# x loaded a second time in turned layout, and the inverse norms spread over rows, in a fused decoder-block kernel

## What is computed

```python
u = rms_norm(h, norm_w[layer])            # x * rsqrt(mean(x*x) + eps) * w
proj = jnp.einsum('bsd,dc->bsc', u, w_in[layer])
hg_q, hg_f, hg_i, hg_z, at_q, at_k, at_v, at_z = jnp.split(proj, split_points, axis=-1)
...
o_hg = hgrn2_mixer(hg_q, hg_f, hg_i, lb); o_hg = rms_norm per head * silu(hg_z)
o_at = mixture of three dilated_window_attention(q, k, v) * silu(at_z)
h = h + einsum(concat([o_hg, o_at]), w_out)
return rms_norm(h, final_norm_w)
```

## Time and profile before

| | us |
|---|---|
| median of 3 runs | 1277.51 |
| lowest, highest | 1275.31, 1278.64 |
| the profiled execution, its own time | 1280.67 |
| its span, first to last instruction | 1278.9 |

### The profile page before, as it was taken

The page is one execution under the profiler, slowest core; times in us unless marked ns, Lnnn a source line. Parts: engine busy times, 40 slices in busy tenths (PEclk is TensorE's granted clock), DMA queues, the critical chain, the costliest instruction groups (busy, mean ns, idle before and its releaser), DMA issues.

```text
span 1278.9 us, 24337 instructions
## 1 busy us (share of the span) xinstructions
PE 1248.3 (98%) x8944; PEld 1090.0 (85%) x8944; DVE 704.3 (55%) x1933; ACT 460.3 (36%) x1328; POOL 436.2 (34%) x441
## 2 busy tenths in 40 slices
PE   7999999999999999999999999999999998999997
PEld 7989999999999989999888888888888876888886
DVE  5847877887766797111455444544554545333332
ACT  5631222222222212112555555554554546421121
POOL 5543254343534413122153345333533434021000
PEclk8999999999999999999999999999999998999999
DMA  6520122211221212341455466545545666544431
GB/s 213 175 90 19 55 63 81 77 59 59 63 79 59 75 67 76 96 116 48 125 141 141 122 143 152 134 116 148 147 125 140 161 179 181 160 145 143 148 116 66
DMA packets 121717, 143.94 MB, mean 113 GB/s; under 512 B 20352, under 2 KB 86400, under 8 KB 121600
## 3 DMA queue, kind: packets, MB, share of 16 engines
q1 hardware_dynamic: 117024, 134.26, 36.9%
q10 hardware_dynamic: 4576, 8.13, 2.3%
HBM read 87.56 MB, written 29.62 MB: 92 GB/s over the span
## 4 chain that ended last, share of the span: by engine, by line
PE 88%; DVE 3%; DMA 3%; issue 1%; POOL 1%; ACT 1%; SPq 1%; ACTq 0%; POOLq 0%; DVEq 0%
PE bank L665 11%; PE bank L667 11%; PE bank L666 11%; PE bank L837 6%; PE bank L836 6%; PE bank L835 6%; PE bank L863 5%; PE bank L865 5%; PE bank L864 5%; PE bank L927 3%; PE bank L936 3%; PE bank L991 3%; PE bank L998 3%; PE bank L760 2%; PE bank L964 2%
## 5 line engine op out<-in xcount | busy, mean ns | idle before, releaser
L665 PE MATMUL bank<-w_hi,u_hi 128*128 128x256 f32 x768 | 221.3, 288 | 3.3 <-DVE u_lo L1472 2.4
L666 PE MATMUL bank<-w_lo,u_hi 128*128 128x256 f32 x768 | 218.2, 284 | 0.0
L667 PE MATMUL bank<-w_hi,u_lo 128*128 128x256 f32 x768 | 218.1, 284 | 0.0
L665 PEld LDWEIGHTS bank<-w_hi,u_hi 128*128 128x128 f32 x768 | 148.1, 193 | 5.1 <-DVE u_lo L1472 3.9
L666 PEld LDWEIGHTS bank<-w_lo,u_hi 128*128 128x128 f32 x768 | 148.2, 193 | 0.1
L667 PEld LDWEIGHTS bank<-w_hi,u_lo 128*128 128x128 f32 x768 | 148.1, 193 | 0.0
L1472 DVE TENSOR_TENSOR room<-room 128x256 f32<-128x256 f32 (+6 forms) x386 | 130.9, 386 | 16.7 <-POOL room L1357 10.7
L835 PE MATMUL bank<-u_hi,w_hi 128*128 128x512 f32 x256 | 107.8, 421 | 0.5 <-issue 0.5
L1472 DVE TENSOR_TENSOR t<-bank,tab 128x512 f32<-128x512 f32 x64 | 42.4, 684 | 116.6 <-DMA tab<-in_rope 52.7
L836 PE MATMUL bank<-u_lo,w_hi 128*128 128x512 f32 x256 | 101.9, 398 | 2.7 <-DMA far_v<-values 2.7
L665 PE MATMUL bank<-u_hi,w_hi 128*128 128x512 f32 x256 | 103.0, 402 | 0.6 <-ACT sg_tile L1093 0.6
(11 more groups left out here) (169 smaller groups left out, 2846.9 us busy)
## 6 DMA issues: line engine op xcount, KB each, us to landing
qd<-turned SPq DMA_DIRECT2D x64, 256.0 KB, 4.5
stage<-in_w_groups SPq DMA_DIRECT2D x42, 256.0 KB, 4.0
room<-in_x SPq DMA_DIRECT2D x16, 512.0 KB, 3.9
values_gates<-vg_tile SPq DMA_DIRECT2D x64, 128.0 KB, 1.7
room<-values_gates SPq DMA_DIRECT2D x16, 512.0 KB, 3.9
tab<-in_rope SPq DMA_DIRECT2D x16, 512.0 KB, 4.5
wide<-mix_weights SPq DMA_DIRECT2D x32, 256.0 KB, 3.9
xr<-in_x SPq DMA_DIRECT2D x16, 512.0 KB, 4.9
```

The lines of the kernel that those rows point to most:

```text
L665: yield nc.tensor.matmul(dst, lhs_hi(k), rhs_hi(k), start=(k == 0), stop=False)
L666: yield nc.tensor.matmul(dst, lhs_hi(k), rhs_lo(k), start=False, stop=False)
L667: last = nc.tensor.matmul(dst, lhs_lo(k), rhs_hi(k), start=False, stop=(k == KT_N - 1))
```

## The change

The host hands x over a second time, turned: tile by tile, the 128 features of a group over the partitions and 128 positions along the row (`x_turned`). The kernel loads both. x itself is only squared and summed. The turned x goes into three slots `xT` of two tiles each, four tiles one by one (`load_turned`), and the other twelve as pairs of 1 MB (`load_pair`). TensorE no longer turns x. Instead `spread_norms` turns the column of inverse norms of a tile, broadcast to 128 columns, so that each partition gets the whole row of 128 norms in PSUM. VectorE then multiplies turned x in place by the gain of its partition and by that row, eight operations of 128 elements a tile (`scaled`) or eight of 256 a pair (`scaled_pair`). The rounding and the subtraction stay as they were; the high parts of tile 0 are made by VectorE.

The norms are made and spread two tiles at a time, from tile 4 on, and ahead of use. Rows of x and turned x are asked for earlier: a slot of x is free as soon as it is squared (`xsq_done`) and no longer when it is scaled, and a slot of turned x when the low parts of both its tiles are made. The next group's weight pieces are asked for earlier and split later. The bounds of the forget gate are made first of all. TensorE runs 20 and 24 idle transposes instead of 28 and 12.

```diff
-SPLIT_AT = (1, 4, 7, 10)
+XT_SLOTS = 3
+SINGLE = 4
+PAIRS = TILES // 2
+SPLIT_AT = (3, 6, 9, 12)
...
-        xn = [p2.take(D) for _ in range(2)]
+        xT = [p2.take(2, KT_N, P) for _ in range(XT_SLOTS)]
         xsq = p2.take(D)
-        un = [p2.take(KT_N, P) for _ in range(2)]
...
+        def rstd_row(t):
+            if t < SINGLE:
+                return bank[(3, 4, 1, 2)[t]][:, 0:P]
+            return bank[1 + (t // 2 - 2) % 4][:, (t % 2) * P:(t % 2 + 1) * P]
+        def rstd_rows_of_pair(q):
+            return bank[1 + (q - 2) % 4][:, 0:2 * P].rearrange("p (t c) -> p t c", t=2)
...
@@ SyncE
             sp.dma_start(nw[:, :], norm_w).then_inc(const_ready, 16)
+            sp.dma_start(lb_in, lb_logits).then_inc(lb_landed, 16)
+            def load_turned(t):
+                sp.dma_start(xT[t // 2][:, t % 2], x_turned[t].rearrange("p (k c) -> p k c", k=KT_N)).then_inc(xT_single[t], 16)
+            def load_pair(q):
+                sp.dma_start(xT[q % XT_SLOTS].rearrange("p t k c -> p t (k c)"),
+                             x_turned[2 * q:2 * q + 2].rearrange("t p c -> p t c")).then_inc(xT_landed[q % XT_SLOTS], 16)
             load_x(0)
+            load_turned(0)
             load_piece(0, 0)
             load_x(1)
             load_piece(0, 1)
+            load_turned(1)
             for i in (2, 3):
                 sp.dma_start(first_raw(i), w_groups[0, :, 2 * i:2 * i + 2, :]).then_inc(w_first[i - 2], 16)
             load_x(2)
+            load_turned(2)
             load_x(3)
-            sp.dma_start(lb_in, lb_logits).then_inc(lb_landed, 16)
+            load_turned(3)
             sp.dma_start(g_all, gate_g).then_inc(g_landed, 16)
+            for t in range(3):
+                after(xsq_done, t + 1)
+                load_x(t + X_SLOTS)
+                if t == 1:
+                    load_pair(2)
+            load_piece(1, 0)
             sp.dma_start(tri, tri_masks).then_inc(tri_landed, 16)
-            for step in range(TILES + 5):
-                if step >= 5:
-                    phase1_store(0, step - 5)
-                if step - 3 in SPLIT_AT:
-                    load_piece(1, SPLIT_AT.index(step - 3))
-                if step + X_SLOTS < TILES:
-                    after(xn_done, step + 1)
-                    load_x(step + X_SLOTS)
+            for t in range(TILES):
+                if t + 7 < TILES:
+                    after(xsq_done, t + 4)
+                    load_x(t + 7)
+                if t % 2 and t // 2 + XT_SLOTS < PAIRS:
+                    after(ulo_done, t + 1)
+                    load_pair(t // 2 + XT_SLOTS)
+                if t + 2 in SPLIT_AT[1:]:
+                    load_piece(1, SPLIT_AT.index(t + 2))
+                if t >= 1:
+                    phase1_store(0, t - 1)
+            phase1_store(0, TILES - 1)
@@ TensorE
-            def x_transposes(t):
...
+            def spread_norms(t, many):
+                pe.wait_ge(rstd_done, t + many)
+                if t >= SINGLE and (t // 2 - 2) % 4 < 2:
+                    pe.wait_ge(un_done, t // 2 + 1 if t == SINGLE else t - 4 if t > SINGLE + 2 else SINGLE)
+                for z in range(t, t + many):
+                    last = nc.tensor.transpose(rstd_row(z), rstd[:, z:z + 1].to_broadcast([P, P]), ident[:, :])
+                last.then_inc(rows_done, many)
-            idle_transposes(28)
-            x_transposes(0)
-            idle_transposes(12)
-            x_transposes(1)
+            idle_transposes(20)
+            spread_norms(0, 1)
+            idle_transposes(24)
+            spread_norms(1, 1)
             for t in range(TILES):
-                if 1 <= t < TILES - 2:
-                    x_transposes(t + 2)
                 pe.wait_ge(ulo_done, t + 1)
                 matmuls = phase1_tile(0, t, "prologue")
-                if t == 0:
-                    run(itertools.islice(matmuls, 16))
-                    x_transposes(2)
+                run(itertools.islice(matmuls, 16 if t == 0 else 12))
+                if t < 2:
+                    spread_norms(t + 2, 1)
+                elif t < 4:
+                    spread_norms(2 * t, 2)
+                elif t % 2 == 0 and t + 5 < TILES:
+                    spread_norms(t + 4, 2)
                 run(matmuls)
@@ ScalarE
+            act.wait_ge(lb_step, 2)
+            nc.scalar.activation(lb_in, lb_in, ACT.Exp).then_inc(lb_step, 1)
+            square(0)
+            split_hi(0, 0, 0)
+            square(1)
+            for i in range(1, PIECES):
+                split_hi(0, i, 0)
+            square(2)
+            for t in range(1, TILES + 2):
+                if t == 2:
+                    phase1_tile(0, 0, "prologue")
+                if t < TILES:
+                    high_parts(t)
+                for z in {4: (6, 7), 5: (8, 9)}.get(t, (t + 2 if t < 4 else t + 4,)):
+                    if z < TILES:
+                        square(z)
+                if t >= 3:
+                    phase1_tile(0, t - 2, "prologue")
@@ GpSimd
+            def inverse_norms(t, many):
...
+            inverse_norms(0, 1)
+            split_lo(0, 0, 0)
+            inverse_norms(1, 1)
+            for i in range(1, PIECES):
+                split_lo(0, i, 0)
+            inverse_norms(2, 1)
+            inverse_norms(3, 1)
...
+            for t in range(2, TILES + 2):
+                if t in (3, 4, 5):
+                    inverse_norms(2 * t - 2, 2)
+                elif t >= 7 and t % 2 and t + 4 < TILES:
+                    inverse_norms(t + 3, 2)
+                phase1_tile(0, t - 2, "prologue")
@@ VectorE
+            def scaled_pair(q):
+                slot = xT[q % XT_SLOTS]
+                dve.wait_ge(xT_landed[q % XT_SLOTS], 16 * ((q - 2) // XT_SLOTS + 1))
+                dve.wait_ge(rows_done, 2 * q + 2)
+                for k in range(KT_N):
+                    last = nc.vector.scalar_tensor_tensor(out=slot[:, :, k, :], in0=slot[:, :, k, :], scalar=nw[:, k:k + 1],
+                                                          in1=rstd_rows_of_pair(q), op0=ALU.mult, op1=ALU.mult)
+                last.then_inc(un_done, 2)
+            for t in range(SINGLE):
+                scaled(t)
+                if t == 0:
+                    dve.wait_ge(un_done, 1)
+                    nc.vector.tensor_copy(u_hi[:, :, 0:P], xT[0][:, 0]).then_inc(uhi_done, 1)
+                low_parts(t)
+            scaled_pair(2)
+            for q in range(2, PAIRS):
+                if q == 2:
+                    low_parts(4)
+                    low_parts(5)
+                if q + 1 < PAIRS:
+                    scaled_pair(q + 1)
+                if q > 2:
+                    low_parts(2 * q)
+                    low_parts(2 * q + 1)
@@ host
+        "x_turned": np.asarray(x)[0].reshape(TILES, P, KT_N, P).transpose(0, 3, 2, 1).reshape(TILES, P, D),
```

133 lines of the change are left out of this document (47 added, 86 removed).

## The result

The changed kernel is slower. Its median over four executions is 1285.32 us (1284.47 to 1288.42) against 1276.70 (1275.31 to 1278.64) of the kernel before beside it: ratio 1.0071, 95% interval 1.0048 to 1.0094. Run again later, beside more executions of before, it took 1283.74 against 1278.00: 1.0049 (1.0030 to 1.0068). So 6 to 9 us are lost, where I forecast 2 won. The profiled execution took 1288.42 us, its span 1286.6, against 1280.67 and 1278.9.

What follows compares the result with a forecast made beforehand. TensorE bounds the kernel; second rows at 38.1 + products 36.0 + rows 1.3 + clock 1.6 + low-part waits 3.1 + sigmoid 0.5 = 80.6 against 82.54, 2.0 us won: 1275.5 us, range 1270.5 to 1280.0.

Steps and rivals of the forecast that it cites:

- The bound and the removed work: TensorE, busy 98% of the span, bounds the kernel; 10.3 us of transposes of x leave its path in the opening stage.
- The start: Opening microseconds: tile 0 starts at 14.5 instead of 15.7 and ends at 20.4 against 22.5, 2.1 us won.
- Two waits: TensorE stands for inverse norms within tiles 2 and 3, 3 and 5 us, because of the order of ScalarE's work.
- The rest of the stage: From the second rows of norms at 38.1 to the last sigmoid's end at 80.6: products, rows, clock, low parts, sigmoid.
- the loads: DMA queue in the opening stage: the remaining 18.35 MB at 406 GB/s last until 55.2, early enough for the last pair.
- the price of the rows: Sixteen transposes on TensorE spread the inverse norms, 0.1 us each plus 0.08 lateness; 1.3 us for the last eight.
- the 300 products: TensorE's products from 38.1 to the opening stage's end, at 0.12 us each: 36.0 us.
- waits for low parts: TensorE waits for VectorE's subtractions later in the opening stage: 3.1 us, four of 0.8, bounded by 1 and 5.
- 6.5 us in hand for the last pair: Margin between the end of the loads at 55.2 and the time the last pair of turned x is wanted, 61.7.
- the slower rival: The DMA queue becomes the bound at 319 GB/s; stage ends at 86.3, 3.8 us late, 1281.3 in all; chance 0.12.
- Everything after that point is the same program ... shifted along: Behind tile 15's sigmoid both kernels run the same program paced by TensorE, so nothing is gained or lost there.
- the tests that I named for wrong: Signs of error: no pause over 1 us, tiles 10 to 15 waiting for turned x, a changed run after 83.

Runs made afterwards that it cites:

- e3_squares: The changed kernel with ScalarE's squares 4 to 9 moved one place ahead in its list; 1285.62 us, ratio 1.0066 to the kernel before.
- g2_light: The changed kernel without the row loads of x for tiles 8 to 15, which the result needs; 1281.67 us, ratio 1.0034 to the kernel before.
- e6_waits: The kernel before with 60 long-met waits (30 more instructions) on TensorE ahead of its idle transposes; 1280.58 us, ratio 1.0036.
- g1_delay: The kernel before with TensorE waiting for the first tile of x ahead of its idle transposes; 1276.87 us, ratio 1.0002.

## Why the prediction was wrong

**The bound and the removed work: right.** The 128 transposes are gone, TensorE is busy 7.3 us less, and the fused operations cost what I took: 2.15 us for eight of 128 (2.2), 3.22 for eight of 256 (3.2).

**The start: 1.4 us off.** Tile 0 started at 14.26 (14.5). The row of tile 2 came at 19.65, not 18.7, as GpSimd's power took 1.40 us instead of 0.55 (from 18.20, while VectorE subtracted until 19.19), and the eight products behind it ran at half clock: tile 0 ended at 21.8 instead of 20.4.

**Two waits: right in place and cause.** 3.63 and 3.71 for 3 and 5, ended by the inverse norms, at 31.4 and 39.7 for 30.3 and 38.1. That ScalarE's list sets them was right too; but e3_squares, which all but removes them, won 2.0 us of their 7.3, since TensorE then waited for the sigmoids in the same list.

**The rest of the stage: 3.5 us off, and "the loads" is the step that failed, beside the price of the rows.** From the second rows to the end took 46.0 us where I had 42.5. TensorE's timeline gives the terms, taken and measured: the 300 products 36.0 and 35.8; half clock 1.6 and 1.6; the last sigmoid 0.5 and 0.8; waits for low parts 3.1 and 5.0; rows of norms 1.3 and 2.8. In g2_light, where no pair was late, the waits for low parts came to 2.9: that term was right for loads in time, and the loads put the 2 us on it. The rows are the second miss. I priced them by TensorE's work alone, without a wait, and three of them waited for GpSimd, whose small operations ended only behind VectorE's subtractions.

The sum had 6.5 us in hand for the last pair, since it let 18.35 MB go at 406 GB/s without a pause. The rate was right as long as only loads ran. But the queue stood half empty from 30 to 40 us, because SyncE's list puts a pair behind a row that waits for a square: I counted bytes and did not walk SyncE's list, although the prediction walked the other lists. From 40 us on, loads mixed with stores ran at 320 GB/s for a share of 0.94, which is 340 for a full queue. That is the slower rival's mechanism, at the rate from which I said it decides (345): reading the share of 0.58 as an honest one would have given 319, nearer than my 406. The last pair was scaled from 68.86; my 61.7 was the wish, the rival's 68.6 the landing. The page of the Trainium skill (DMA: Bandwidth & Descriptors, "Where 436 GB/s comes from") had 358 GB/s; 410 and 401 over twenty microseconds, with this one core at work, speak against it for loads alone, and for the mixture it is nearer to the 340 than my 406.

**"Everything after that point is the same program ... shifted along": wrong, and nearly as large a part.** It is the same program, but by the medians it took 3 to 5 us longer, and no step of mine had a price for that: I put it at nothing because the instructions are the same. What took the time stays open. That a change of TensorE's list by some instructions without work can cost as much is shown in the kernel before; that it is the cause here is not, as restoring the places returned 0.7 to 2.0 us. Of the 226 instructions that the diff takes off TensorE's list I priced the work and not the number.

Stage and rest together: 5.1 us missed in the stage (1.6 up to the second rows, 3.5 behind), 3 to 5 behind it. Two of the tests that I named for wrong hit: a stage after 83 that does not run as before, and tiles 10 to 15 waiting for turned x (pairs 5 to 7, 7.5 us on VectorE).

## What to carry to other kernels

Walk the list of the engine that issues the DMAs like any other: a load whose slot is free does not start while one in front of it waits for something else, and bytes by rate hide such a hole. Take the rate for a mixture of loads and stores from a stretch that has that mixture, corrected by its share. And before believing or disbelieving a difference of 0.3% between two long programs, add some thirty instructions without work to TensorE's list of the faster one: if that alone costs as much, as 30 to 128 instructions did here (2 to 4.5 us of 1277), a difference of this size can't be put down to what the edit does. Take a second profile of the same program as well before reading a few microseconds out of one.

## What the runs showed of the hardware

- An instruction packet of 16 KB took 0.9 to 1.7 us in the changed kernel, 71 times, and where one began 1.4 to 2.0 us ahead of a product that needed a load of 128 KB, the product came 0.9 to 1.5 us late (seven profiles).
- A wait that is long met costs TensorE 0.11 us: 30 such instructions moved its first transpose from 3.34 to 6.64, 128 to 17.21.
- A GpSimd operation on two numbers a partition took 0.19 us alone and 1.46, 2.00 and 1.86 us beside VectorE's subtraction of two SBUF tiles, each time until 0.05 us behind its end (changed kernel, 48.91, 57.13, 65.34).
- With the first idle transposes lasting until 12.6 us and the second until 14.8 (e6_waits, g1_delay) the granted clock stayed at full level through tile 0; in before, with the second until 11.5, it was at half from 15.0 to 21.8. The stage ended only 0.4 us earlier by it.
